# Reordered first loads, an output projection by column halves, early closed banks and a paired final norm in a one-core transformer block

## What is computed

```python
mod = silu(c) @ w_ada + b_ada                    # six vectors; mod_c from c_ctx alike
h   = modulate(rms_norm(x, norm_attn), sh1, sc1) # and hc from ctx
dq, dk, dv, sq, sk, sv = split(h @ w_in)         # rotary on the queries and keys of x
out = concat(head_rms(diff_attention) * 0.8, head_rms(window_attention)) @ w_out
x   = x + g1 * out
h2  = modulate(rms_norm(x, norm_ffn), sh2, sc2)
s   = scores of (h2 @ w_q) with sub_keys         # top 16 of 128 twice, then 16 of 256
act = gelu(h2 @ u.T)                             # the selected of 16384 experts
y   = (gate * act) @ v
return rms_norm(x + g2 * y, final_norm)
```

## Time and profile before

| | us |
|---|---|
| median of three runs (2185.06 to 2189.71) | 2186.73 |
| the profiled execution | 2179.53 |
| its span, first to last instruction | 2177.7 |
| TensorE busy | 2089.6 (96%) |
| VectorE busy | 1674.4 (77%) |
| ScalarE busy | 1223.7 (56%) |
| GpSimd busy | 310.3 (14%) |

### The profile page before, as it was taken

The page is one execution under the profiler, slowest core; times in us unless marked ns, Lnnn a source line. Parts: engine busy times, 40 slices in busy tenths (PEclk is TensorE's granted clock), DMA queues, the critical chain, the costliest instruction groups (busy, mean ns, idle before and its releaser), DMA issues.

```text
span 2177.7 us, 42186 instructions
## 1 busy us (share of the span) xinstructions
PE 2089.6 (96%) x13442; PEld 1848.0 (85%) x13442; DVE 1674.4 (77%) x2955; ACT 1223.7 (56%) x2243; POOL 310.3 (14%) x264
## 2 busy tenths in 40 slices
PE   3899999899999999999999999999999999999997
PEld 0478888667999999999999999999888778788786
DVE  5377767697666478878878588778688898988986
ACT  2332234486344477677776555655566666666664
POOL 0000000000000000000000211111334564322320
PEclk7899999899999999999999999999999999999999
DMA  9878876500565545555589644445689999999991
GB/s 385 336 282 284 280 261 234 189 1 1 205 243 190 172 155 186 180 182 184 183 294 365 210 157 161 154 157 183 244 306 363 357 358 347 334 364 354 389 337 69
DMA packets 160909, 524.75 MB, mean 241 GB/s; under 512 B 34976, under 2 KB 35792, under 8 KB 160208
## 3 DMA queue, kind: packets, MB, share of 16 engines
q1 hardware_dynamic: 123840, 452.63, 58.2%
q0 software_dynamic: 20576, 67.20, 8.9%
q10 hardware_dynamic: 16432, 4.19, 0.9%
HBM read 515.52 MB, written 8.39 MB: 241 GB/s over the span
## 4 chain that ended last, share of the span: by engine, by line
PE 88%; DVE 5%; DMA 4%; issue 1%; ACT 1%; SPq 0%; DVEq 0%; ACTq 0%
PE PS L790 71%; PE PS L1103 9%; DMA raw<-stream 2%; PE PS L1047 2%; DMA ada_t<-w_ada 2%; PE PS L946 1%; DVE st L1341 1%; PE PS L920 1%; PE PS L833 1%; DVE w_lo L1140 1%; PE PS L797 1%; PE PS L773 1%; PE PS L934 1%; ACT w_hi L438 1%; DVE mixed L1662 0%
## 5 line engine op out<-in xcount | busy, mean ns | idle before, releaser
L438 ACT ACTIVATE w_hi<-raw 128x512 fp32r<-128x512 f32 x1088 | 683.3, 630 | 691.9 <-PE PS L790 552.2
L1140 DVE TENSOR_TENSOR w_lo<-raw,w_hi 128x512 fp32r<-128x512 f32 x1088 | 734.1, 690 | 337.1 <-ACT w_hi L438 321.4
L790 PE MATMUL PS<-h_h,w_hi 128*128 128x256 f32 (+1 forms) x2304 | 658.1, 286 | 3.1 <-DVE h_l L1170 2.1
L790 PE MATMUL PS<-h_h,w_lo 128*128 128x256 f32 (+1 forms) x2304 | 653.1, 283 | 0.0
L790 PE MATMUL PS<-h_l,w_hi 128*128 128x256 f32 (+1 forms) x2304 | 653.0, 283 | 0.0
L790 PEld LDWEIGHTS PS<-h_h,w_hi 128*128 128x128 f32 x2304 | 443.4, 192 | 4.2 <-issue 2.6
L790 PEld LDWEIGHTS PS<-h_l,w_hi 128*128 128x128 f32 x2304 | 443.5, 193 | 0.0
L790 PEld LDWEIGHTS PS<-h_h,w_lo 128*128 128x128 f32 x2304 | 443.1, 192 | 0.0
L790 PE MATMUL PS<-w_hi,p_hl 128*128 128x512 f32 x1024 | 400.1, 391 | 7.3 <-DVE w_lo L1140 7.0
L790 PEld LDWEIGHTS PS<-w_hi,p_hl 128*128 128x128 f32 x1024 | 192.6, 188 | 51.5 <-issue 10.9
L1103 PE MATMUL PS<-w_hi,p_hl 128*128 128x512 f32 x512 | 199.8, 390 | 0.0
(11 more groups left out here) (228 smaller groups left out, 2834.0 us busy)
## 6 DMA issues: line engine op xcount, KB each, us to landing
raw<-stream SPq DMA_DIRECT2D x544, 512.0 KB, 4.0
raw_far<-stream SPq DMA_DIRECT2D x104, 512.0 KB, 6.8
ada<-w_ada SPq DMA_DIRECT2D x96, 512.0 KB, 4.4
ada_t<-w_ada SPq DMA_DIRECT2D x64, 512.0 KB, 9.3
ada_u<-w_ada SPq DMA_DIRECT2D x32, 512.0 KB, 5.6
values_scratch<-A ACTq DMA_DIRECT2D x1, 2560.0 KB, 19.0
x_c<-x_ctx SPq DMA_DIRECT2D x1, 2048.0 KB, 7.6
x<-x_lat SPq DMA_DIRECT2D x1, 2048.0 KB, 15.0
```

What stands on the lines that cost most here:

```text
L438: nc.scalar.activation(w_hi[:, (2 * j + hf) % SPLIT, :], ring[:, j, hf * HALF:(hf + 1) * HALF], ACT.Copy).then_inc(S["w_high"], 1)
L790: ins = mm(out_, l_, r_, start=(start and q == 0), stop=(stop and q == 2), skip_group_check=check)
L1140: V_.tensor_tensor(w_lo[:, h % SPLIT, :], ring[:, h // 2 % RAW, at_:at_ + HALF], w_hi[:, h % SPLIT, :].bitcast(F32), ALU.subtract).then_in ...
```

## The change

- Front: three of the small loads (b_ada, norms, ident) have their own semaphore mod_in and are issued behind the eighth tile of w_ada; the other seven stand behind tile 23. The first three pairs of units are issued before tiles 16, 28 and 44 instead of 24, 40 and 56. The second square sum stands behind tile 15 instead of tile 19.
- Queries: VectorE's two ropes of a query chunk have a unit's split between them. TensorE makes the small products and the third turn, then the first scores, and then the last turn.
- Output projection: w_out is read by column halves, so that banks 0 to 3 are complete after half of it. VectorE adds the first eight residuals and pairs of squares in the second half. The closings have one column instead of 512. The small products come before the sum of squares, which takes the first eight tiles in two products.
- Scaling before the query projection: a tile's low part is made one step earlier.
- Query projection: each pair of banks is closed and copied by itself.
- Values: the first tile's products open the banks, the last one's close them; the first p_high and p_low come before the last gelu's use. The far row's addresses are made behind them.
- Tail: the banks are copied as they end; ScalarE loads its square-root table ahead of the squares and multiplies x3 by the norm's weights; three pair sums of squares on VectorE; four output multiplications of 128x1024.

The core of the diff:

```diff
@@ first loads (SyncE)
             ada1(1)
+            for dst, src in MOD_LOADS:
+                sp.dma_start(dst, src).then_inc(S["mod_in"], 16)
             ada1(2)
-            for dst, src in SMALL_LOADS[1:]:
-                sp.dma_start(dst, src).then_inc(S["par_in"], 16)
             ada1(3)
+            for a in range(4, 16):
+                if a in (4, 7, 11):
+                    u = 2 * (4, 7, 11).index(a)
+                    unit(u // 4, u % 4, first=u < 4)
+                    unit(u // 4, u % 4 + 1, first=u < 4)
+                if a == 6:
+                    for dst, src in SMALL_LOADS[1:]:
+                        sp.dma_start(dst, src).then_inc(S["par_in"], 16)
+                ada1(a)
@@ output units (SyncE)
+            def out_unit(n):
+                b, j = (U_OUT + n) // RAW, n % RAW
+                row = U_OUT + 2 * (n % KT) + n // KT if n < N_OUT else U_OUT + n
@@ queries (TensorE)
-            turn_queries(3)
+            pe.wait_ge(S["evac_d"], EVAC_DC[8])
             ada_columns(4, 4, acc)
+            turn_queries(2)
...
-            pe.wait_ge(S["turn_q_kept"], 8)
+            pe.wait_ge(S["turn_q_kept"], 6)
             score_pair(0)
+            turn_queries(3)
+            pe.wait_ge(S["turn_q_kept"], 8)
@@ closing (TensorE)
-            def close_banks():
-                for k in range(8):
-                    ins = mm(PS[:, k, :], zeros[:, 0:P], zeros_bank, start=False, stop=True)
+            def close_banks(ks=range(8)):
+                for k in ks:
+                    ins = mm(PS[:, k, 0:1], zeros[:, 0:P], zeros[:, 0:1], start=False, stop=True)
@@ output projection (TensorE)
+            with pe.Fori(0, 4) as b:
+                out_block(b, 18, 0)
+            close_banks(range(4)).then_inc(S["attn_out"], 1)
+            with pe.Fori(0, 3) as b:
+                out_block(b, 22, 1)
+            out_block(3, 22, 1, last=True)
+            close_banks((6, 7)).then_inc(S["attn_out"], 1)
@@ query projection (TensorE)
+                    if last and h >= 4:
+                        close_banks((2 * (h - 4), 2 * (h - 4) + 1)).then_inc(S["qp_done"], 1)
@@ values (ScalarE)
+            routed_turn(63, first_values)
+            p_high(1, 1)
@@ residual (VectorE)
+            for q in range(4):
+                out_turn(2, q)
+                dve.wait_ge(S["attn_out"], 1)
+                residual(2 * q)
+                residual(2 * q + 1)
+            for q in range(4):
+                out_turn(3, q, lows=q < 3)
+                if q:
+                    add_squares(2 * q)
@@ tail (ScalarE, VectorE)
+            nc.scalar.activation(early[:], eps[:], ACT.Sqrt)
...
+                if k in (5, 7, 9):
+                    add_squares(k - 3)
...
+            for g in range(4):
+                ks = slice(4 * g, 4 * g + 4)
+                dve.wait_ge(S["x3_scaled"], 4 * g + 4)
+                V_.tensor_tensor(ot[:, ks, :], x3n[:, ks, :], rstd[:].unsqueeze(1).broadcast_to([P, 4, T]), ALU.mult
+                                 ).then_inc(S["tail_y"], 4)
```

320 lines of the change are left out of this document (200 added, 120 removed).

## The result

Beside the kernel before on the same chip, the changed kernel took 2156.45 us (median of four runs, 2148.60 to 2161.68) where the kernel before took 2185.89 (four runs, 2184.12 to 2189.71): a ratio of 0.986, with a 95% interval of 0.9825 to 0.9895. It is 29.4 us faster; 30.8 had been forecast, and a time of 2156. In two later jobs, each on a chip of its own, the same two kernels stood at 2146.8 and 2179.8 us (0.984, 0.9826 to 0.9853) and at 2146.8 and 2180.0 us (0.985, 0.9837 to 0.9863), 33 us apart. The four runs of the changed kernel in the first comparison spread over 13 us, its five in each later job over 2.0 and 2.5.

A forecast was written before the change was run, and what follows sets the result against it. TensorE was taken as busy for 2089.6 of 2177.7 us, leaving mainly handovers to win. Seven terms sum to 30.8 us: 2179.53 becomes 2148.7, plus 7.2 for the median gives 2156 us, range 2148 to 2171.

The forecast's parts named there:

- Front, -9.0: First loads and second square sum earlier: last w_ada products start at 105.8 us instead of 114.87; 9.0 us saved.
- rival (a): Front: DMA engines run dry between two groups and most of the gain goes back; 24.8 us in all, 2162; chance 0.17.
- Ropes, -2.6: Query projection's chunk changes: a split between VectorE's two ropes shortens TensorE's w_lo wait, 1.3 us saved twice (0 to -3.2).
- Handover, -6.0: Query projection to attention: small products, third turn and first scores run under the last ropes; 6.0 us saved (4 to 7).
- Rival (b): Transposes and short sums fall to 1.2 GHz: handover gives 4.5 us, output projection and tail less; 2160; chance 0.10.
- Output projection, -4.9: Column halves put residuals and squares under the projection, so the first query product comes earlier; 4.9 us saved (3.5 to 6).
- rival (c): Output projection's second half: VectorE becomes the bound, late splits stop TensorE, 9 us lost; 2165; chance 0.06.
- Query projection, -1.6: End of query projection: paired closings and copies under the last four halves replace closing and waiting; 1.6 us saved (1 to 2.4).
- Value opening, -0.8: Start of values: first product near 1554.8 instead of 1556.13 us; part may be given back; 0.8 us saved (0 to 1.3).
- Tail, -5.9: Behind the last value product: earlier copies, shorter sum, four output multiplications, earlier table load; 5.9 us saved (4.5 to 7).
- Rival (d): Straight code behind loops at four places: fetching it stops TensorE and the kernel is slower; 10 us each gives 2196; chance 0.04.
- Rival (e): Tail and handovers: another wait ends last in each, so only half of the sum is won; 2171; chance 0.08.

The follow-up runs named there:

- second profile of the changed kernel: The changed kernel, unchanged, run and profiled once more beside the kernel before: 2146.80 us against 2179.76, span 2145.1.
- The parts timed alone: The kernel before with one part of the change each: tail 0.9981, front 0.9951, handover 0.9954, both projections 0.9944 of its time.
- first and third job: First: changed kernel 2146.80 us, value opening undone 2148.24, gathers later 2155.03, tail alone 0.9981. Third: changed 2146.76, p_hl half earlier 2143.47, gathers spread 2145.46, both 2142.54.
- second job: Kernel before with front (0.9951), handover (0.9954) or projections (0.9944) alone; changed kernel with first p_hl part half a unit earlier (0.9843); one chip.

## Why the prediction was right, and where not

The forecast time was met to 0.5 us. The terms of the sum were all within 1 us of what the stretches show, so the mechanism was right; that the time came out so close is luck in part, as told below. In the terms of the sum, against the stretches of the table:

1. **Front, -9.0.** The last w_ada product comes at 108.2 to 111.3 us in ten profiles and at 116.5 to 119.0 in four with the old order: -8.4 by the means. The first projection came at 48.9 to 50.0 (48.5 forecast). The last six tiles began at 105.0 in the first profile, sooner than the 105.8 forecast, and then waited for transfers. The step that was a little off is "the DMA engines then never run dry": from 48.9 to 85 us they moved 406 to 412 GB/s, but 315 from 90 to 95 and 344 from 95 to 100, and 417 behind. That is rival (a) in small, and the term lost 0.6 us by it and not 6.
2. **Ropes, -2.6.** -3.0, and no wait for w_lo between 350 and 400. The step "the seventh 0.2 us late" was too careful, nothing was late in any profile with the edit.
3. **Handover, -6.0.** -6.2 by the means of the two groups (129.7 against 135.9). The first scores were forecast 3.9 us behind the projection's end and came 3.6 behind it. The stretch to the first maximum is 6.4 us, with 6.5 forecast. Rival (b) does not fall, though. The granted clock is 1.00 in the 6.4 us themselves, but the lower level came soon behind in nine of the ten profiles with the edit, in one of them at 405.5, within the handover. That one was 4.4 us under the mean of the old code, where rival (b) had said 4.5: it came true in one execution of ten, and not in the measured one. The Trainium skill has a rule by which transposes don't count for the clock ("TensorE: Matmul & The Clock Gate", Part 4: PE-mode transpose). The 40 transposes at full clock speak against it; the handover can't settle it, because one-column products, scores and waits lie between its transposes.
4. **Output projection, -4.9.** -5.5 behind it in every kernel that has the edit, less what the six closings that now lie inside cost it, 0.34 us in all (0.5 was taken): -5.1. The first query product stands 10.5 us behind the projection's end, 10 was forecast. The two first profiles are 6.3 us apart over the projection and the stretch behind it; 1.2 of that is the clock, which was low for 5.1 us of the projection before and for 2.3 after. TensorE is busy for 93.65 of 93.65 us, so rival (c), VectorE as the bound with more in its queue, falls.
5. **Query projection, -1.6.** -2.3. The step that failed is the delay by the last pair: 64 products with the sub-keys take 7.39 us without a stop, as before (7.38), so the scores of the other pairs cover its copy wholly. Of the -3.8 that the two first profiles show, 1.5 is the low clock at the old kernel's start.
6. **Value opening, -0.8.** -1.3 to the first product, and by two profiles and one against it about 0 once the value phase is counted. "Part may be given back" was right and too weak. The first product stood 2.04 us behind the last of u, and the forecast (1554.8, with that product at 1552.80) had 2.0. What the forecast did not say is that 1.76 of these are a wait for p_hl's low part on VectorE, which could be had for the move of one half unit.
7. **Tail, -5.9.** -5.4. The sum ended 13.7 us behind the last value product (13.6 forecast), the end came after 24.2 (24 forecast).

The sum of the measured terms is 8.4 + 3.0 + 6.2 + 5.1 + 2.3 + 0 + 5.4 = 30.4 us; the times say 33 on two chips. Between the profile of before and the second profile of the changed kernel, whose spans are 32.6 us apart, the stretches account for the rest: the output projection and the query projection were 2.2 and 1.5 us longer before for their time at the lower level, less 1.1 that the values lost and some tenths elsewhere. The runs fit that, with a mean granted clock of 0.981 to 0.988 for the kernel before and of 0.989 to 0.992 for the changed one in these two jobs, but that the clock is the whole of the 2.6 in the medians is not shown. The parts timed alone come to 10.7 + 10.1 + 12.3 + 4.1 = 37 us by their ratios. The closings behind the values, 1.6 us, are in two of them, and with intervals of 2 to 3.5 us either way on each, the rest by which they pass the whole is not told from nothing.

Where luck comes in: the forecast had 2148.7 us for the profiled execution and put 7.2 on top for the median. The profiled execution took 2154.3, 5.6 more: 8.5 us in the value phase that no term had, less some 3 that the other stretches gained beyond the sum. The median stood only 2.2 above it. The offset of 7.2 was no property of the kernel: on the chips of the first and third job the kernel before ran at 2179.8 and 2180.0, where its profile had stood (2179.53). Two errors of 5 us, one each way, gave 2156.

Rival (d), code loading behind the straight blocks: the page counts 30 transfers (0.49 MB) in the instruction queue, three more than the page of before, and at none of the four places does TensorE stop but for the wait on p_hl. Rival (e) falls: each part did what it says, though the value opening gave its gain back.

## What to carry to other kernels

When an engine is busy for 96% of the span, the time left lies in handovers, and each can be priced by itself by following which instruction ends last; closings, copies, table loads and partial sums that can run while the last products still do cost next to nothing there, and a plain list of such steps added up to within 3 us of the measured difference. Look at the start of the next stage before you count a gain: here the earlier opening of the values was worth nothing by the end of the stage. And compare a stage in several profiles, of several chips if that can be had, before a wait in it is put down to the change: here one profile each would have blamed it for 8.5 us that kernels with the old value code lose too. Count the time at the lower clock in each stage before you compare two lengths; in a stage without waits it explained every tenth.

## What the runs showed of the hardware

- **Chips, or their states, differ by 9 us.** The kernel before took 2179.8, 2180.0 and 2189.05 us on three chips, and 2185.89 in the first comparison. In the changed kernel's first profile and in all four of the second job, TensorE waits twice 12 to 21 us behind its first value product, while GpSimd's first gathers are under way, and in each the value phase lasts 599 us or more. ScalarE waits there for a buffer whose last product had ended, by TensorE's timeline, 3 to 9 us earlier. Which signal or transfer is late there, and why only in these five profiles, stays open.
- **The clock after a wait is not settled by the wait's length.** After 2.14 us before the query projection the products ran at 1.2 GHz in the profile of before, and at 2.4 in those of three other kernels with the same wait; after the 1.76 us before the values at 1.2 in the changed kernel's first profile (0.63 us a product) and at 2.4 in its second (0.39). Such stretches cost 1.5 to 3 us each and move between executions.
- **What a us at the lower level costs.** In the output projection, where TensorE never waits, each us at 1.2 GHz made it 0.44 us longer, in fourteen profiles with 0 to 5.4 such us.
- **A table load and the instruction behind it.** The load took 1.28 us, and the next instruction of ScalarE started 0.02 us behind it, so that it cost 1.3 us in all in the tail.
- **A one-column product that closes a bank** costs TensorE 0.06 to 0.07 us inside a stream (0.34 us for the six of the output projection, 0.14 a pair in the query projection), against 0.22 for one of 512 columns, of which eight in a row took 1.90.
